# A mixture of experts with 160 slots for each expert in place of 192

## The reference

```python
def moe_swiglu(x, w_router, b_router, w1, w3, w2):
    ...
    logits = (xt @ w_router).astype(jnp.float32) + b_router.astype(jnp.float32)
    top_v, top_i = lax.top_k(logits, TOP_K)
    gates = jax.nn.softmax(top_v, axis=-1)
    ...
    for e in range(N_EXPERTS):
        y = y + dense_gate[:, e:e + 1].astype(x.dtype) * swiglu(xt, w1[e], w3[e], w2[e])
```

## Time and profile before

| | us |
|---|---|
| median of 3 runs (lowest, highest) | 2535.13 (2534.64, 2539.26) |
| span of the profiled execution | 2533.3 |
| TensorE busy in that span | 2451.1 (97%) |
| VectorE, ScalarE, GpSimdE busy | 1753.3, 1056.2, 607.0 |

### The profile page before, as it was taken

One profiled execution on the slowest core, in us unless ns is written; L12 is line 12 of the kernel. 1 busy time (PEld: TensorE's weight loads), 2 busy tenths in 40 slices (PEclk: granted clock), 3 DMA queues, 4 the chain that ended last, 5 costly groups with the idle time before them and its releaser, 6 DMA issues. The chain is left out here.

```text
span 2533.3 us, 40965 instructions
## 1 busy us (share of the span) xinstructions
PE 2451.1 (97%) x15775; PEld 2023.4 (80%) x15775; DVE 1753.3 (69%) x2889; ACT 1056.2 (42%) x1586; POOL 607.0 (24%) x495
## 2 busy tenths in 40 slices
PE   8999999999999999899999999999999999999998
PEld 6788887788887889799999999887676577767576
DVE  7945666468987757767666676674887666688567
ACT  4444323321221352555555455534444454244453
POOL 2404221430240331244233442340023000024001
PEclk9999999999999999899999999999999999999999
DMA  4321002336553757467777777844222213322121
GB/s 158 96 82 41 2 3 67 120 136 203 166 180 111 211 163 266 147 226 250 225 252 239 233 249 225 276 153 152 71 80 61 73 59 100 94 80 72 33 84 67
DMA packets 265197, 348.87 MB, mean 138 GB/s; under 512 B 23184, under 2 KB 221008, under 8 KB 264400
## 3 DMA queue, kind: packets, MB, share of 16 engines
q1 hardware_dynamic: 250272, 301.24, 36.8%
q0 software_dynamic: 9136, 30.28, 3.5%
q10 hardware_dynamic: 5632, 15.21, 1.8%
HBM read 323.37 MB, written 20.71 MB: 136 GB/s over the span
## 5 line engine op out<-in xcount | busy, mean ns | idle before, releaser
L3247 PE MATMUL ps<-x_feat_r,moe_w_hi 128*128 128x384 f32 x1408 | 405.2, 360 | 1.1 <-DVE x_feat_r L3359 1.1
L2754 DVE TENSOR_TENSOR moe_w_lo<-ring,moe_w_hi 128x2048 fp32r<-128x2048 f32 x144 | 315.4, 2191 | 128.5 <-ACT moe_w_hi L2749 128.4
L3250 PE MATMUL ps<-x_feat_r,moe_w_lo 128*128 128x192 f32 x1408 | 353.1, 251 | 0.0
L2749 ACT ACTIVATE moe_w_hi<-ring 128x2048 fp32r<-128x2048 f32 x144 | 254.9, 1770 | 95.1 <-PE ps L267 75.1
L3250 PEld LDWEIGHTS ps<-x_feat_r,moe_w_lo 128*128 128x128 f32 x1408 | 269.0, 191 | 0.3
L3247 PEld LDWEIGHTS ps<-x_feat_r,moe_w_hi 128*128 128x128 f32 x1408 | 264.3, 188 | 2.2 <-issue 1.9
L271 PE MATMUL ps<-x_free_r,ring_r 128*128 128x512 f32 x496 | 195.7, 395 | 0.0
L270 PE MATMUL ps<-ring_r,x_feat_r 128*128 128x256 f32 (+2 forms) x576 | 184.3, 320 | 0.0
L267 PE MATMUL ps<-x_feat_r,ffn_w_hi 128*128 128x512 f32 x352 | 139.3, 396 | 1.2 <-DVE ffn_w_lo L2697 1.2
L271 PE MATMUL ps<-x_feat_r,ffn_w_lo 128*128 128x512 f32 x352 | 139.4, 396 | 0.0
L270 PE MATMUL ps<-x_free_r,ffn_w_hi 128*128 128x512 f32 x352 | 138.5, 393 | 0.0
(11 more groups left out here) (676 smaller groups left out, 6448.5 us busy)
## 6 DMA issues: line engine op xcount, KB each, us to landing
ring<-in_moe_w SPq DMA_DIRECT2D x120, 1024.0 KB, 5.5
ring<-in_w_in SPq DMA_DIRECT2D x32, 1024.0 KB, 5.2
ring<-in_ffn_w SPq DMA_DIRECT2D x30, 1024.0 KB, 6.3
ring<-in_gdn_w_in SPq DMA_DIRECT2D x12, 1024.0 KB, 5.8
ring<-in_ada_t SPq DMA_DIRECT2D x24, 512.0 KB, 3.9
cond_w<-in_ada_t POOLq DMA_DIRECT2D x24, 512.0 KB, 6.2
ring<-in_moe_w SPq DMA_DIRECT2D x24, 512.0 KB, 3.8
ring<-in_s_w_glu SPq DMA_DIRECT2D x8, 1024.0 KB, 8.4
```

Source lines behind the costliest of these rows:

```text
L2749: self.prog.nc.scalar.activation(self.flat(self.hi, j % SPLITS, j), self.raw(j), ACT.Copy).then_inc(self.hi_done, 1)
L2754: self.prog.nc.vector.tensor_tensor(self.flat(self.lo, j % SPLITS, j), self.raw(j), self.flat(self.hi, j % SPLITS, j).bitcast(F32), ALU.su ...
L3247: mm = nc.tensor.matmul(out, wh[:, k, cs], both[:, k, :], start=(k == 0), stop=False)
L3250: mm = nc.tensor.matmul(out[:, 0:SLOTS], wl[:, k, cs], xg[0][:, k, :], start=False, stop=(k == KD - 1))
```

## The change

SLOTS becomes 160, so there are 32 late slots. Their hidden units are kept once, in plain float32 (`hid_late`), and multiplied with the raw weight tiles in plain float32: the two halves of the features and the two rows of a tile go to four groups of 32 columns of the array, all in one bank, and VectorE adds the groups afterwards. As the down-projection now reads the raw tile, that is held longer: there are six rooms (four in the ring, two in a buffer that is free in this stage), and the room of a down tile is given back by TensorE (`raw_used`) and not by VectorE's split. The late results are stored by two DMAs, and the last expert's placing uses half of the array's rows for the late part. The diff, cut to its core:

```diff
-SLOTS = 192
-SLOT_PAD = 256
+SLOTS = 160
+LATE = SLOTS - P
+ROOMS = 6
...
+        if self.raw_used is not None and j >= N_UP:
+            sp.wait_ge(self.raw_used, values[j])
+        else:
+            sp.wait_ge(self.lo_done, values[j])
...
-                ahead = j + RAW
+                ahead = j + self.rooms
...
-    late, lower = slice(0, LATE), slice(LATE, P)
-    S_ = PartStream(prog, st, EXPERTS, w1, w3, w2, hi, lo)
+    late, quadrants = slice(0, LATE), [slice(q * LATE, (q + 1) * LATE) for q in range(4)]
+    LATE_BANK = 6
+    S_ = PartStream(prog, st, EXPERTS, w1, w3, w2, hi, lo, more)
...
-                    for i in range(4):
-                        cs = slice((i % 2) * BANK, (i % 2 + 1) * BANK)
-                        if i < 2:
-                            mm = three_pass(nc, ps[:, 4 + i, :], (hid_hi[:, m, 0:P], hid_lo[:, m, :]), (wh[:, r, cs], wl[:, r, cs]),
-                                            m == 0, m == FT - 1, S_.leave if r == 0 and i == 0 else None)
-                        else:
-                            nc.tensor.matmul(ps[:, 4 + i, :], hid_hi[:, m, P:], wh[:, r, cs], start=(m == 0), stop=False)
-                            mm = nc.tensor.matmul(ps[:, 4 + i, :], hid_hi[:, m, P:], wl[:, r, cs], start=False,
-                                                  stop=(m == FT - 1))
+                    for h, cs in enumerate(halves):
+                        mm = three_pass(nc, ps[:, 4 + h, :], (hid_hi[:, m, 0:P], hid_lo[:, m, :]), (wh[:, r, cs], wl[:, r, cs]),
+                                        m == 0, m == FT - 1, S_.leave if r == 0 and h == 0 else None)
+                w = S_.raw_view(j)
+                for h, cs in enumerate(halves):
+                    for r in rows:
+                        m = 2 * (j - N_UP) + r
+                        mm = nc.tensor.matmul(ps[quadrants[2 * h + r], LATE_BANK, :], hid_late[:, m, :], w[:, r, cs],
+                                              start=(m < 2), stop=(m >= FT - 2))
+                mm.then_inc(S_.raw_used, 1)
```

More of the change, by code:

```diff
@@ L2662, with __init__ @@
 class PartStream:
-    def __init__(self, prog, st, parts, w1, w3, w2, hi, lo):
+    def __init__(self, prog, st, parts, w1, w3, w2, hi, lo, more=None):
         self.prog, self.parts, self.w = prog, parts, (w1, w3, w2)
         self.hi, self.lo = hi, lo
-        self.landed = [st.counter(f"landed_{i}") for i in range(RAW)]
+        self.more, self.rooms = more, RAW if more is None else ROOMS
+        self.landed = [st.counter(f"landed_{i}") for i in range(self.rooms)]
+        self.raw_used = None if more is None else st.counter("raw_used")
         self.hi_done, self.lo_done = st.counter("hi_done"), st.counter("lo_done")
@@ L2713, in flat, with room, raw_view @@
         return buf[:, slot, 0:k * n]
+    def room(self, j):
+        at, (k, n) = j % self.rooms, tile_rows(j)
+        if at < RING:
+            return self.prog.weights.ring[:, at, 0:k * n]
+        return self.more[:, at - RING, 0:k * n]
     def raw(self, j):
-        return self.flat(self.prog.weights.ring, j % RAW, j)
+        return self.room(j)
+    def raw_view(self, j):
+        return self.room(j).rearrange("p (k n) -> p k n", n=tile_rows(j)[1])
     def load(self, sp, e, j):
@@ L2725, in load @@
             src = w2[bass.ds(e, 1), r * P:min(r + 2, FT) * P, :]
-        sp.dma_start(self.view(self.prog.weights.ring, j % RAW, j), src.rearrange("a (k p) n -> p (a k) n", p=P)
-                     ).then_inc(self.landed[j % RAW], 16)
+        sp.dma_start(self.raw_view(j), src.rearrange("a (k p) n -> p (a k) n", p=P)
+                     ).then_inc(self.landed[j % self.rooms], 16)
     def loads(self, sp):
@@ L3126, in sparse_parts, with home_of @@
     nc, ps = prog.nc, prog.ps
[L3127 to L3128 removed]
+    rows_in, y, moved, hid_hi, hid_lo, hid_late, sig, prod, total, cross, hi, lo, pick, token, spot, home = buf
+    more = prog.x_free.rearrange("p k n -> p (k n)").rearrange("p (a n) -> p a n", a=ROOMS - RING)
+    def home_of(t):
+        return (rows_in, y)[t // 2][:, t % 2, :]
     both = prog.x_hi[:, :, 0:2 * SLOTS]
@@ L3169, in x_piece, with late_rows @@
             return xg[part][:, 4 * i:4 * i + 4, 0:P], ps[:, i, :].rearrange("p (k n) -> p k n", n=P)
-        return xg[part][:, :, P:SLOTS], ps[:, 2, :].rearrange("p (k n) -> p k n", n=LATE)
-    def y_late_part(rows):
-        return ps[rows, 6:8, :]
+        return xg[part][:, :, P:SLOTS], ps[:, 2, 0:KD * LATE].rearrange("p (k n) -> p k n", n=LATE)
+    def late_rows(h):
+        return slice(2 * h * LATE, 2 * (h + 1) * LATE)
     def wide(x):
@@ L3210, in turn_pick @@
                 nc.tensor.transpose(ps[:, 6, cs], pick[:, t, 0:P].bitcast(F32), prog.ident)
-                for rows in (late, lower):
+                for rows in quadrants:
                     m = nc.tensor.matmul(ps[rows, 7, cs], pick[:, t, P:SLOTS].bitcast(F32), prog.ident, start=True, stop=True)
@@ L3492, in expert @@
                 return
[L3493 to L3498, removed]
+            pool.wait_ge(y_early, e + 2)
+            pool.sem_inc(storing, 1)
+            pool.dma_start(prog.y_rows[bass.ds(e, 1), 0:P, :].rearrange("a s n -> (a s) n"), y[:, 0, :]).then_inc(stored, 16)
+            pool.wait_ge(y_late, e + 2)
+            pool.sem_inc(storing, 1)
+            for h in range(2):
+                pool.dma_start(prog.y_rows[bass.ds(e, 1), P:SLOTS, h * BANK:(h + 1) * BANK].rearrange("a s n -> (a s) n"),
+                               y[quadrants[2 * h], 1, 0:BANK]).then_inc(stored, 16)
+            pool.wait_ge(stored, e * 48 + 48)
             pool.sem_inc(y_free, 1)
@@ L3565, in program @@
                     if i == 4:
-                        late = slice(0, SLOTS - P)
+                        late = slice(0, LATE)
                         for dst, at in ((rows_in[:, 0, :], spot[:, 0:1]), (rows_in[late, 1, :], spot[late, 1:2])):
```

84 lines of the change are left out of this document (50 added, 34 removed).

## The result

The changed kernel takes **3414.9 us** (median of 4 runs, 3412.9 to 3416.6) against 2534.9 (4 runs on the same chip, 2534.6 to 2539.3): the ratio is 1.346, with a 95% interval of 1.344 to 1.348. The forecast was 3405, with a range of 3360 to 3435. The span grew from 2533.3 to 3412.6, by 879.3 us.

The account below looks back on a forecast made before the run. TensorE, busy 97% of the span, was taken as the bound. Start, eight dense parts, pauses, clock and tail end the stage at 2577.4 against 1707.3, +870.1 us on the 2535.1 median: 3405 us, range 3360 to 3435.

Parts of the forecast that it names:

- The branch: Router's flag: fullest expert's 176 tokens exceed 160.5, so all engines take the dense form, every expert computing all 512 tokens.
- The products: Dense form on TensorE: 184.27 us per part, read from the first layer's dense FFN; eight parts take 1474.2 us.
- Rival (c): Dense form with 512-column products at the skill's pace instead of 0.233 us: 107 us less, 3298 us; chance 0.01.
- The start: Start of the expert stage: first product at 1064.1, 1.3 us earlier than before; half clock then costs 1.8 us.
- The pauses: Dense form: 1.0 us in each part's middle, eight times, 8.0; 3.2 us between parts, seven times, 22.4.
- The clock: Pauses between parts: a clock fall costs 1.7 us; half of the seven taken, 6 us, bounds 0 and 12.
- The bounds of 2.0 us a part: Upper bound for reading code of a branch and loop not run before: 2.0 us per part, +16 in all.
- (a): Slot form is taken, four column groups at once: 2470 us, faster, between 2428 and 2504; chance 0.13.
- (b): Slot form is taken, but the down-projection's column groups run in turn: 2580 us, slower; chance 0.02.
- the gain of the pairs in the up-projections: Slot form's up-projections: a pair takes 0.26 us instead of 0.29, 42 us on 1408 pairs.
- the block of late products: Slot form's down-projection: 1.21 us for 1.85 on five tiles, 1.21 for 0.93 on one; 23 us in all.

Follow-up runs that it names:

- experiment 1: The kernel before with only the flag's threshold changed from SLOTS + 0.5 to 160.5, slot code left at 192 slots: 3417.8 us, ratio 1.347.
- experiment 4: The kernel before with 176 slots in place of 192, down-projection kept with two groups of 64 columns, 48 filled: 2514.6 us, ratio 0.992.
- experiment 3: The changed kernel with the next part's tile 0 split before the additions and the down-projection begun bank by bank: 3371.6 us, ratio 1.329.
- experiment 6: The kernel before with 160 slots, its old down-projection and three rooms, slot form forced, rows beyond an expert's 160th left out: 2498.2 us, ratio 0.985.

## Why the prediction was right, and by how much its terms were off

**The branch.** The step that decided, 176 tokens against a threshold of 160.5, holds: trace and experiment 1 show it, and experiment 4 brackets the count, as a threshold of 176.5 lets the slot form run.

**The products.** 184.27 us for a part, from the FFN, is right: experiment 3, which takes the pauses away, has it to the hundredth. In the changed kernel the last part, from 2397.68 to the end of its last product's turn (2584.60 + 0.23), takes 187.15, which is 184.27, a middle of 1.2 and a fall of some 1.5 to 1.7. The up-projections of a part without a fall at its start:

```profile
1448.14:1572.00 123.86, 123.34 (x528) 99.12 (x528) 35.38 (x23) 26.56 (x23) 40.74 (x20) 1.00 0.31 102
```

Apart from the pauses TensorE never waits for weights, with DMA at 31%. Rival (c) fell: at 216 ns a product the 528 would take 114 us. That figure was from the Trainium skill ("TensorE: Matmul & The Clock Gate", section Back-to-back issue gap), which gives it for the gap of a single product; neither the FFN nor this stage agrees with it, and the measurement decides.

**The start** was 2.6 us too early: 1064.1 forecast, 1066.71 measured. 0.8 is the flag, which came later; 1.28 is the ACT_TABLE_LOAD ahead of ScalarE's first split, a term that the sum left out; the last 0.5 is the first subtraction, 2.5 for 2.29, and hand-overs that take 0.3 longer than was put. In the earlier trace rows the slot form's first split has none right ahead of it; in the dense form it stands between the landed rows and the split, on the path. The Trainium skill ("ScalarE: Activation LUTs", section What ACT_TABLE_LOAD costs) gives 1283 ns for such a load, and the row agrees; the section adds a drain of about 1380 ns for a switch of sets, which the rows don't show: the split starts 1.29 us after the load did.

**The pauses.** Middle and between parts were put at 1.0 + 3.2 a part and measure 4.75 (189.0 - 184.27): the waits themselves, 1.10 and 3.18, are as forecast, and the excess is in what surrounds them: the first product behind each pause takes 0.1 longer to the next, and L3015 with its two columns stands behind the last product. Eight times, some 4 us.

**The clock.** "Half of them", 6 us, was a bet between 0 and 12: five of seven fell, at 1.5 each, 7.5. That the bet came so near is luck: experiment 1, with the same seven pauses, had four. The start's half clock lasted 4.4 us for 3.6 and cost 1.9 for 1.8.

Together 2.6 + 4.1 + 1.5 + 0.1 = 8.3 more than the sum's 870.1, for 878.2 measured; the 1.1 behind the stage is the rest of the span. The bounds of 2.0 us a part for the code of a branch not run before weren't needed: the terms above leave nothing of that size.

**The rivals.** (a)'s price, 2470, was 2474 on the chip; (b)'s 2580 was refuted. Of (a)'s terms the gain of the pairs in the up-projections was put a little high (42 for 38.6 in eight experts' turns, experiment 6); the block of late products was right.

## What to carry to other kernels

A constant that sizes a buffer and also guards a fallback must be held against the data before anything in the rewritten code is priced: here 16 tokens too few in one expert cost 880 us, and sizing by the fullest expert (176) gained 21 us of span, 19 of them in the experts, where sizing by the array's groups (160) could not be used. That margin belongs to these inputs: one more token in that expert would send the 176-slot kernel to the dense form too. A fallback that a trace never shows can often be read from the same function run elsewhere, with its pauses priced one by one from what stands ahead of the late instruction on its engine's queue.

## What the runs showed that was not expected

Seven pauses of 3.18 us, all alike, were followed by a half clock of 3.4 us in five cases and not in two. It isn't the place in the program that sets them apart. Experiment 1 has the same seven pauses of 3.18 us, and there the clock fell behind the second, third, fifth and sixth, where the changed kernel's fell behind the first, third, fourth, sixth and seventh. Its windows behind the second pause (end at 1448.44) and the first (end at 1259.47):

```profile
1449.30:1452.70 3.40, 3.40 (x10) 0.50 0.89 254
1259.50:1266.00 6.50, 6.50 (x28) 1.00 0.82 266
```

So a pause of this length costs 1.5 us more or doesn't, from execution to execution; the traces of these two kernels show 9 falls in 14. What decides it was not tried.

Raw tiles as operands cost buffers, not time on the engine: the same down-projection is 23 us faster than the old one with six rooms and 22 us slower with three. Of the 45 us between, more than a third is clock and not wait.
